# The first block's mixing in one weight stream, with gates and branches inside the attention rounds

## The reference

```python
h = rms_norm(x, norm_mix_pre_g)
mq, mk, mv, dq, dk, dv, ga, gb = split(h @ w_in)      # six parts of 512 columns, two gates of 1024
ya = moba_attention(mq, mk, mv)      # 8 heads of 64, causal, softmax with linear position bias
yb = diff_attention(dq, dk, dv)      # 4 heads: softmax(q1 k1) - lam * softmax(q2 k2), values of 128
yb = rms_norm(yb, diff_subln_g) * (1 - lam_init)
merged = sigmoid(ga) * (ya @ w_branch_a) + sigmoid(gb) * (yb @ w_branch_b)
x = x + rms_norm(merged @ w_out, norm_mix_post_g)
# ... feed-forward; then the second block: a modulation vector silu(c) @ w_ada (6144 columns),
# gated linear attention (GLA), dilated attention, w_out_2, feed-forward
```

## Time and profile before

| | |
|---|---|
| median of 3 runs | 1617.15 us (1614.07 to 1618.74) |
| the profiled execution | 1614.58 us, of which the span of the trace is 1612.9 us |
| start to the first attention round | 0 to 46 us |
| eight attention rounds | 46 to 360 us |
| gate rounds | 360.2 to 481.6 us |
| w_out | 481.6 to 525.4 us |
| PE, DVE, ACT, POOL busy | 92%, 52%, 35%, 15% of the span |

### The profile page before, as it was taken

One profiled execution on the slowest core, in us unless ns is written; L12 is line 12 of the kernel. 1 busy time (PEld: TensorE's weight loads), 2 busy tenths in 40 slices (PEclk: granted clock), 3 DMA queues, 4 the chain that ended last, 5 costly groups with the idle time before them and its releaser, 6 DMA issues.

```text
span 1612.9 us, 19938 instructions
## 1 busy us (share of the span) xinstructions
PE 1484.6 (92%) x6744; PEld 1176.3 (73%) x6744; DVE 838.6 (52%) x1346; ACT 567.9 (35%) x920; POOL 236.1 (15%) x178
## 2 busy tenths in 40 slices
PE   6888877769999899999999799889978999999999
PEld 3676655548888588888888478757656888888887
DVE  6556466664334554444422567645554665655321
ACT  4332323332224432223322443344423544444211
POOL 0778866660000000000000000000000000000000
PEclk9989878889999999999999899999989999999999
DMA  3433323313222122223333111111102222223332
GB/s 138 164 131 136 136 99 117 106 51 104 100 95 88 43 100 97 98 91 104 100 100 95 61 53 53 65 41 39 65 14 88 78 91 99 96 92 103 108 95 88
DMA packets 39092, 146.02 MB, mean 91 GB/s; under 512 B 4352, under 2 KB 4624, under 8 KB 39056
## 3 DMA queue, kind: packets, MB, share of 16 engines
q1 hardware_dynamic: 34448, 120.39, 22.4%
q0 software_dynamic: 4608, 25.17, 4.5%
HBM read 143.44 MB, written 2.10 MB: 90 GB/s over the span
## 4 chain that ended last, share of the span: by engine, by line
PE 82%; DVE 10%; issue 4%; POOL 2%; ACT 2%; DVEq 0%; DMA 0%; POOLq 0%; SPq 0%; ACTq 0%
PE bank L527 67%; PE bank L651 3%; PE bank L562 2%; PE bank L577 2%; PE bank L640 2%; PE bank L786 1%; PE bank L549 1%; DVE prob L1365 1%; DVE w_lo L1239 1%; POOL ada L388 1%; DVE prob L1424 1%; DVE cur_q L1394 1%; POOL ada L385 1%; DVE nlam L1423 1%; DVE prob L1426 1%
## 5 line engine op out<-in xcount | busy, mean ns | idle before, releaser
L527 PE MATMUL bank<-h_hi,w_hi 128*128 128x512 f32 x1176 | 482.7, 410 | 9.7 <-DVE h_lo L1264 7.0
L527 PE MATMUL bank<-h_lo,w_hi 128*128 128x512 f32 x1176 | 467.0, 397 | 0.0
L527 PE MATMUL bank<-h_hi,w_lo 128*128 128x512 f32 x1176 | 466.5, 397 | 0.0
L1239 DVE TENSOR_TENSOR w_lo<-raw,w_hi 128x1024 fp32r<-128x1024 f32 (+1 forms) x225 | 285.5, 1272 | 242.4 <-ACT w_hi L866 241.2
L866 ACT ACTIVATE w_hi<-raw 128x1024 fp32r<-128x1024 f32 (+1 forms) x225 | 233.5, 1039 | 321.6 <-PE bank L527 315.8
L527 PEld LDWEIGHTS bank<-h_hi,w_hi 128*128 128x128 f32 x1176 | 225.9, 192 | 82.2 <-issue 31.0
L527 PEld LDWEIGHTS bank<-h_hi,w_lo 128*128 128x128 f32 x1176 | 226.0, 192 | 49.1
L527 PEld LDWEIGHTS bank<-h_lo,w_hi 128*128 128x128 f32 x1176 | 226.7, 193 | 42.3 <-issue 0.2
L527 PE MATMUL bank<-f_hi,w_hi 128*128 128x512 f32 x352 | 136.9, 389 | 0.0
L527 PE MATMUL bank<-f_lo,w_hi 128*128 128x512 f32 x352 | 136.9, 389 | 0.0
L527 PE MATMUL bank<-f_hi,w_lo 128*128 128x512 f32 x352 | 136.9, 389 | 0.0
(11 more groups left out here) (229 smaller groups left out, 1644.9 us busy)
## 6 DMA issues: line engine op xcount, KB each, us to landing
raw<-in_w_up SPq DMA_DIRECT2D x66, 512.0 KB, 3.2
raw<-in_w_in SPq DMA_DIRECT2D x65, 512.0 KB, 3.3
ada<-in_w_ada POOLq DMA_DIRECT2D x32, 768.0 KB, 4.6
raw<-in_w_down SPq DMA_DIRECT2D x32, 512.0 KB, 3.6
raw<-in_w_gate SPq DMA_DIRECT2D x22, 512.0 KB, 3.3
raw<-in_w_out SPq DMA_DIRECT2D x16, 512.0 KB, 3.3
raw<-in_w_down SPq DMA_DIRECT2D x16, 384.0 KB, 3.2
raw<-in_w_branch SPq DMA_DIRECT2D x8, 512.0 KB, 3.3
```

What stands on the lines that cost most here:

```text
L527: last = pe.matmul(to[:, :], wt[:, slot, k, :], act_[:, rhs0 + k, :], start=(k == first and n == 0), stop=(k == K - 1 and n == 2))
L1239: dve.tensor_tensor(w_lo[:, s, 0:K, :], raw[:, s, 0:K, :], w_hi[:, s, 0:K, :].bitcast(F32), ALU.subtract).then_inc(split_ready[s], 1)
```

## The change

The mixing is written anew; everything from w_out on stays, but for two reorderings.

- **One weight stream.** 48 units (w_mix) in the order of their use through the three slots. The first eight are the values of all heads, computed with tokens on the partitions (value_products: the activations are the stationary operand, the weights the moving one of 512 columns) into v_moba and v_diff. They use x times gain before the norm is known; the norm's factor is turned by four small products (turn_rstd) and applied when the banks are stored. The sum of squares is accumulated by GpSimd.
- **Rounds.** Rounds 0 to 7 hold 4, 4, 4, 4, 5, 5, 4, 4 units: q and k of the next pair, gates (g) and branch a tiles (a). The last four units, branch b, follow the rounds.
- **Values and outputs.** A pair's product with the values is made in one go, turned at once (pair_values: 4 or 8 products of 512 to 128 columns into O0), a round later. The turns of v and of the outputs are gone. For diff heads the squares over the partitions are summed by one product (pair_squares).
- **Gates.** Sigmoid is made of exp, add 1, reciprocal. Gated branch a waits in ma.
- **Modulation.** The tiles of ada are 128 x 8 x 64 and there are two of them in a third of the memory; a chunk is twelve steps. w_ada is laid out in tiles of 64 columns. Modulation of chunk i stands at the end of round i.
- **Second block.** In GLA, DVE's chunk_gate(c) moves behind the state of chunk c+1. Before the last dilated attention PE waits for the third y tile only where it is used, and DVE clears sqacc after that attention. Two masks (seen, dist2) are built during w_out.

```diff
-                for n in range(4):
+                for n in range(12):
                     buf = n % 2
                     chunk = ada[:, buf, :, :]
                     pool.wait_ge(ada_in[buf], w.next(ada_in[buf]))
...
+            for k in range(KD):
+                pool.wait_ge(sq_g[k % 2], w.next(sq_g[k % 2]))
+                pool.tensor_tensor(sqacc[:, :], sqacc[:, :], sq[:, k % 2, :], ALU.add).then_inc(sq_used[k % 2], 1)
+                pool.wait_ge(sq_used[k % 2], w.next(sq_used[k % 2]))
...
+ROUNDS = [(10, "qkgg", 0), (14, "qkgg", 4), (18, "qkgg", 8), (22, "qkgg", 12),
+          (26, "qkgga", 16), (31, "qkgga", 22), (36, "qkgg", 28), (40, "agga", 32)]
+TURNS = {4: (5, 9, 9, 13, 17, 23), 5: (5, 9, 9, 15, 21, 28)}
...
+            def modulation(i):
+
+                pe.wait_ge(ada_ready, i + 1)
+                pe.wait_ge(ada_out, i + 1)
+                if i >= 5:
+                    pe.wait_ge(o_rs, min(i - 4, 3) if i < 7 else 4)
+                for n in range(6):
+                    last = pe.matmul(O1[:, n:n + 1], ada_flat[:, n * P:(n + 1) * P], ones[:, 0:1], start=True, stop=True)
+                last.then_inc(ada_mm, 1)
...
+            for i in range(8):
...
+                pair_scores(i, 0)
+                pair_scores(i, 1)
+                fill(i, 0, values)
+                if i >= 1:
+                    pair_values(i - 1)
+                pair_scores(i, 2)
+                fill(i, values, scores2)
...
+                turn(i, 0)
+                fill(i, turn0, scores3)
+                pair_scores(i, 3)
...
+                modulation(i)
...
+            for n in range(44, 48):
+                pe.wait_ge(split_ready[n % SLOTS], w.next(split_ready[n % SLOTS]))
...
-            pe.wait_ge(y_ready, w.next(y_ready, times=3))
-            attention("dil", "w_out")
+            pe.wait_ge(y_ready, w.next(y_ready, times=2))
+            attention("w_out")
...
+                if c >= 1:
+                    chunk_gate(c - 1)
                 dve.wait_ge(gn_ready, w.next(gn_ready))
...
                 last.then_inc(gon_ready, 1)
-                chunk_gate(c)
+            chunk_gate(NCH - 1)
```

More of the change, by code:

```diff
@@ L656, in attention @@
                     qk_norm_sums(1)
-                if kind == "diff":
-                    pe.wait_ge(y_f32, w.next(y_f32, ahead=1))
                 pe.wait_ge(yt_tok, w.next(yt_tok, times=2))
@@ L700, in _, with value_products @@
-            gates(first=True)
-            with w.repeat(7, {(siga, 1): 1, (sigb, 1): 1, (m_f32, 1): 1,
-                              **{split_ready[s]: 1 for s in range(3)}}):
-                gates()
-            def two_tiles(hi, lo, read, times, late=None):
-                def pair(late=None):
+            def value_products(n, banks):
+                slot = n % SLOTS
+                pe.wait_ge(split_ready[slot], w.next(split_ready[slot]))
+                for kk in range(2):
+                    k = 2 * (n % 4) + kk
+                    if n < 4:
+                        pe.wait_ge(xg_ready, k + 1)
+                    if n == 3 and kk == 1:
+                        turn_rstd()
+                    for r in range(NT):
+                        for m, (xt, wt) in enumerate(((y_hi, w_hi), (y_hi, w_lo), (y_lo, w_hi))):
+                            last = pe.matmul(banks[r][:, :], xt[:, k, P * r:P * r + P],
+                                             wt[:, slot, 4 * kk:4 * kk + 4, :].rearrange("p a b -> p (a b)"),
+                                             start=(k == 0 and m == 0), stop=(k == KD - 1 and m == 2))
+                last.then_inc(unit_done[slot], 1)
@@ new lines, in turn_rstd @@
+            def turn_rstd():
+                pe.wait_ge(rstd_ready, 1)
+                for r in range(NT):
+                    last = pe.matmul(T0[:, r:r + 1], rstd[0:1, P * r:P * r + P], ones[0:1, 0:1], start=True, stop=True)
+                last.then_inc(rcol_turned, 1)
+            for n in range(3):
+                value_products(n, (S0, S1, O0, O1))
+            pe.wait_ge(const_ready, w.next(const_ready))
+            for g in range(2):
+                w.skip(sq_g[g], 4)
+                pe.wait_ge(sq_used[g], w.next(sq_used[g], times=4))
@@ new lines, in branch_row @@
+            def branch_row(n, half, k):
+                slot = n % SLOTS
+                u = OUTPUTS.index((n, half))
+                if k == 0:
+                    pe.wait_ge(g_free[u % 2], u // 2)
+                for m, (wt, act_) in enumerate(((w_hi, y_hi), (w_hi, y_lo), (w_lo, y_hi))):
+                    last = pe.matmul(G[u % 2][:, :], wt[:, slot, 4 * half + k, :], act_[:, 4 + k, :],
+                                     start=(k == 0 and m == 0), stop=(k == 3 and m == 2))
+                if k == 3:
+                    last.then_inc(unit_done[slot] if half else half_done, 1)
@@ new lines, in _, with two_tiles, pair @@
+            for n in range(44, 48):
+                pe.wait_ge(split_ready[n % SLOTS], w.next(split_ready[n % SLOTS]))
+                late = 3 if n == 44 else 4
+                for half in range(2):
+                    for k in range(late):
+                        branch_row(n, half, k)
+                if n == 44:
+                    pe.wait_ge(yb_ready, 8)
+                    for half in range(2):
+                        branch_row(n, half, 3)
+            def two_tiles(hi, lo, read, times, fresh=None):
+                def pair(fresh=None):
@@ L739, in down @@
                     pair()
[L741 to L744 removed]
+            for g in range(2):
+                pe.wait_ge(g_free[g], 23)
+            two_tiles(m_hi, m_lo, drained, 3, fresh=mix_ready)
             sum_squares()
@@ new lines, in _ @@
+            dve.wait_ge(vec_in, w.next(vec_in))
+            for n in range(2):
+                scaled_lo(2 * n)
+                scaled_lo(2 * n + 1)
+                split_lo(n)
+            for k in range(4, KD):
+                scaled_lo(k)
+            dve.wait_ge(cond_exp, w.next(cond_exp))
+            then(dve.tensor_scalar(cond[:, :], cond[:, :], 1.0, 3e38, ALU.add, ALU.min))
+            then(dve.reciprocal(cond[:, :], cond[:, :]))
+            dve.tensor_tensor(cond[:, :], cond[:, :], cols[:, VEC_AT["c_2"]:VEC_AT["c_2"] + 8], ALU.mult).then_inc(cond_r, 1)
```

982 lines of the change are left out of this document (649 added, 333 removed).

## The result

| | before | after |
|---|---|---|
| median | 1616.29 us | 1627.43 us |
| range of the runs | 1614.07 to 1618.74 | 1626.31 to 1629.69 |
| span of the profiled execution | 1612.9 us | 1626.0 us |
| mean granted clock | 0.958 | 0.944 |

The ratio is 1.0073, with a 95% interval from 1.0055 to 1.0091: the change makes the kernel slower by 0.7%. The time lies inside the range of the prediction, but on the other side of no change from its forecast of 1615.

The account below looks back on a forecast made before the run. GpSimd's twelve-step chunks were taken to bound the rounds; w_out starting 9.6 us later and 11.3 gained in the second block gave -1.7, 1612.9 us profiled, so a median of 1615; range 1596 to 1645.

Parts of the forecast that it names:

- The mechanism: Attention rounds: GpSimd's twelve-step chunk sets the pace, 53.0 us a round against PE's 32 to 35, so PE waits.
- the sign: Whole kernel: signs nearly open, faster 0.40, same 0.27, slower 0.33; the summed change was slightly faster.
- sum of -1.7 us: Profiled execution: w_out starting 9.6 us later and the second block gaining 11.3 give 1612.9 us from 1614.58.
- rival 2: GpSimd at ada_in: loads land late, from 4.6 us on; at 5.1 each step waits 0.46, +38 us, 1653; chance 0.10.
- the central statement: Attention rounds: GpSimd's step costs 4.05 us, not a third of 7.69, so twelve make 48.6 where four made 30.8.
- rival 1: GpSimd's step is cheaper: 1582 with a smaller DMA issue, about 1495 if nothing were fixed; chance 0.14.
- contention 3 x 2.1 + 3 x 2.7 = 14.4: Six rounds: GpSimd loses 2.1 us with four units and 2.7 with five to VectorE's w_lo splits and joins.
- The rival's bound of 5 us a round: Contention in the rounds: each w_lo costs its full 1.2 us, joins too; +21 us, 1636; chance 0.10.
- end 25.2: Four branch b units after the rounds: 22.1 of products, 1.2 lower clock, 1.0 VectorE's list, 0.9 until w_out may write.
- -8.9: GLA: two 3.51 us gstate waits and cold instructions go, so the last projection starts at 1054.1 in place of 1063.02.
- The step before the last attention: Second block: PE's 3.95 us idle goes, it waits for cur_k instead, scores begin at 1173.3; -2.4 us.
- -11.3: Second block: the GLA term of -8.9 and the last attention's -2.4 us together.

Follow-up runs that it names:

- The first run above: The kernel before with only w_ada cut into tiles of 64 columns, twelve steps a chunk in place of four: 1729.3 us against 1613.5, ratio 1.0711.
- the first kernel with spread modulations: The changed kernel with modulations 0 to 3 in every second round and 4 to 7 between FFN products (4, 4, 13 iterations): 1534.6 us, ratio 0.9510.

## Why the prediction was wrong

The mechanism was right and the sign was not. What it gave as a sum of -1.7 us was +13.1, and all of the difference lies in few terms.

**What held.** The step of GpSimd, 4.05 us forecast and 4.03 measured, with its DMA at 0.58. The modulation of round 0 ended at 99.1 for 98.7. First product at 9.75 for 10.6. PE idle 15 to 21 us in front of the six products in rounds 1 to 6 (5.9 in the last), distances of 52.7 to 55.7, PE busy for 60 to 71% of a round. w_out itself took 43.8 us in both, so the masks cost nothing. The loads of 256 KB landed in 3.0 us (median; 2.7 to 4.9). One of them at least passed rival 2's 4.6, but GpSimd's only wait for one was 3.7 us in front of the very first multiply, so the wait at every step that the rival feared did not come. By the page the prediction named, the Trainium skill's "DMA: Bandwidth & Descriptors", section "Anatomy of one DMA — SWDGE (gpsimd) path", a load of that size takes 2.6 (an estimate from its formula); the median here is 0.4 above it, and the rule's result, no wait, is what happened. The first run above settles the central statement on its own: the tile width is worth +116 us in a kernel where nothing else changed. The run with two steps gives the other half: PE's new round is 33.4 us (forecast 32 to 35), and with ten twelfths of GpSimd's chain left out the kernel is at 1488.7, where rival 1 had put 1495. Rival 1 itself did not happen, since the step cost what was forecast.

**First failed step: "contention 3 x 2.1 + 3 x 2.7 = 14.4".** Seven chunks took 374.7 us, end to end, for 367.3 forecast, so 7.4 more: 5.9 in the six full ones and 1.5 in the last. By the distances the six full chunks lost 6 x (54.1 - 50.7) = 20.5 us where 14.4 was put. The reasoning behind the small value was that a w_lo "falls into the 1.28 without arithmetic" more often. The share of time in arithmetic does fall, but that stretch (1.23 us as measured) is no longer than a split (1.23), and of the 26 splits in rounds 1 to 6 none lies wholly between two pieces of arithmetic; 18 met an addition. Nor does a short piece lose less: the 64-column additions that a split met took 1.17 us on average, the others 0.33. The run without splits shows their worth: 19 us. The rival's bound of 5 us a round was high, the forecast's value too low.

**Second failed step: "end 25.2".** It was 31.4. The prediction costed VectorE's list for two outputs at its busy time and did not follow what each queue waits for: SP's list has w_up ahead of w_out, and VectorE's list has w_out's split ahead of the evacuation. That is the one place where a load, not arithmetic, held PE (4.56 us). The other part is the clock: PE was busy for 25.6 us of the stage, at 0.90, where the prediction had 22.1 + 1.2 = 23.3. So the 6.2 are 4.6 for this wait, 1.1 ahead of w_out, 0.2 of small waits and 2.3 of slower products, less the 1.9 that the prediction had for idle time. And the wait was worth little by itself: with it gone, the median is 1 us lower, within the spread of the runs, where some 5 were expected, because idle time ahead of w_out and colder products took its place.

**Third: "-8.9" in GLA.** The last projection did come 9.2 us earlier. The term stopped there, at its start. Its 24 products then run at the lower clock, because the waits before it moved right in front of it. These windows of the same 24 products, before and after, are the whole of it (the clock is the column behind the last bracket, 1.00 and 0.79):

```profile
1063.02:1069.66 6.64, 6.64 (x27) 4.91 (x27) 2.96 (x3) 1.44 (x4) 0.00 (x0) 1.00 0.42 127
```

```profile
1077.33:1085.54 8.21, 8.21 (x27) 6.05 (x27) 2.96 (x3) 1.43 (x4) 0.00 (x0) 0.79 0.36 128
```

8.21 for 6.64 is 1.6 us given back. The step before the last attention was -2.5 for -2.4: PE waits 3.4 us there for VectorE's cur_q.

Together: 0.4 (round 0) + 7.4 (contention) + 6.2 (end) = 14.0 of the mixing's 23.6 - 9.6, and of -11.3 in the second block -10.5 came: 14.0 + 0.8 = 14.8, the difference between -1.7 and +13.1.

**Where PE's gain went.** Measured apart, the parts of the change are worth +116 (narrow tiles, alone) and -125 (all the rest, with GpSimd out of the way). They don't add to the +14 that the kernel shows, and could not, since the second was taken with most of GpSimd's steps left out. With the narrow tiles in both, the rest is worth 1627 - 1729 = -102 us (98 between the two profiled spans). The start, 14 us earlier, brings nothing of it: the first modulation begins at 97.7 in both traces, held by GpSimd's first chunk with the narrow tiles alone (23.43 us of waiting) and by PE's own round 0 in the kernel after, and the last one ends at 471.1 and 473.8. What is gained is the gate stage of 121 us, for which 31.4 us of branch b are left (w_out starts at 505.2 in place of 593.4), because its products now lie under GpSimd's chunks, where they cost nothing, and the 10 us of the second block. While each round ends in a modulation of twelve steps, the start and PE's shorter rounds can't show. What the change lacked was a shorter chunk, as the run with two steps shows, or distance between GpSimd's chunks and PE's rounds: with the same 12 steps a chunk, and the sums placed where they are ready, all but some 12 us of the hidden gain comes out (ratio 0.9301 against 0.9217). The new mixing with tiles of 192 columns was not run, so whether four steps a chunk would have done the same in the rounds is not shown.

## What to carry to other kernels

Before work on the busiest engine, look for the engine that is joined to it once a round and count that one's steps with all that is fixed in them: a cut into narrower tiles keeps the columns and multiplies the gaps and DMA issues. If a slow side computation is needed only much later, don't tie it to the fast loop's rounds; give it places to hand over that lie further apart than its own chunk takes there, and read the time of one iteration from a trace before placing them. A wait removed near a stage's start may come back as a cold clock, so price a term to the end of the stage it leads into.

## What the runs showed of the hardware

- GpSimd needs 1.23 us from an addition's end to its next multiply when a DMA issue with a computed address lies between (0.65, then 0.58), the same for 256 KB as before for 768 KB (0.66 and 0.59). In the last chunk, whose addresses are fixed, the 0.65 is 0.30.
- A VectorE subtraction of two SBUF tensors (1.23 us) beside GpSimd additions of 0.32 to 0.8 us stretches these by up to 1.1 us, and costs VectorE 0.18 us on average at 54 us a round. In denser rounds it was more: at 38.4 us a round the additions average 0.73 where 0.59 is undisturbed, and in the first kernel with spread modulations 0.85 over all chunks (0.69 in the kernel after):

```profile
L482 POOL TENSOR_TENSOR ada<-ada 128x256 f32<-128x256 f32 x192 | 163.1, 849 | 15.1
```

- The granted clock was lower behind each of the six waits of 15 to 21 us (0.80 over a round of 54 us in which PE was busy for 32.55), and the first products after shorter ones ran slow too: 0.77 us behind 2.69 us of idle time, where 0.39 is the usual duration. With 13.5 us of waits for GpSimd in five rounds, the longest 5.3, the same products kept PE busy for 18.0 us more.
